# An S5 layer's start reordered: input loaded and squared first, phases rounded through PSUM, turns moved up, Toeplitz products behind all projections

## What is computed

```
def s5_mixer(u, h0, a_re, a_im, log_dt, b_re, b_im, c_re, c_im, d_skip, w_glu):
    lam = lax.complex(a_re, a_im)
    dt = jnp.exp(log_dt)[:, None]
    lam_bar = jnp.exp(lam * dt)
    b_bar = ((lam_bar - 1.0) / lam)[..., None] * lax.complex(b_re, b_im)
    uf = u.reshape(bsz, t_len, SSM_GROUPS, SSM_GROUP)        # u = rmsnorm(x, g_mix)
    bu = einsum('btgh,gph->btgp', uf, b_bar)                 # complex
    if h0 is not None:
        bu = bu.at[:, 0].add(lam_bar * h0)
    _, h = lax.associative_scan(_ssm_combine, (a, bu), axis=1)
    y = einsum(h.real, c_re) - einsum(h.imag, c_im)          # back to 16 channels per group
    y = y.reshape(bsz, t_len, D_MODEL) + d_skip * u
    z = jax.nn.gelu(y)
    gl = z @ w_glu
    return gl[..., :D_MODEL] * jax.nn.sigmoid(gl[..., D_MODEL:]), h[:, -1]
```

## Time and profile before

| | us |
|---|---|
| median of 3 runs | 1636.94 |
| the runs | 1636.31 to 1640.3 |
| profiled execution, as a whole | 1638.2 |
| its span | 1636.4 |

### The profile page before, as it was taken

One profiled execution on the slowest core, in us unless ns is written; L12 is line 12 of the kernel. 1 busy time (PEld: TensorE's weight loads), 2 busy tenths in 40 slices (PEclk: granted clock), 3 DMA queues, 4 the chain that ended last, 5 costly groups with the idle time before them and its releaser, 6 DMA issues.

```text
span 1636.4 us, 23515 instructions
## 1 busy us (share of the span) xinstructions
PE 1510.4 (92%) x8247; PEld 1287.5 (79%) x8248; DVE 1252.6 (77%) x1522; ACT 996.3 (61%) x1299; POOL 121.1 (7%) x142
## 2 busy tenths in 40 slices
PE   2589989999888879999998999998999999999995
PEld 1578989999776868888887888887888888888884
DVE  7844555554656459999987989987999988999993
ACT  3443444433455337777765777766777777777772
POOL 3971103000100000000000000000000000000000
PEclk9589999999988979999999999999999999999997
DMA  2004579544422219999987999987999988999980
GB/s 101 26 1 162 185 130 314 184 170 180 155 102 110 78 51 362 362 364 354 359 321 295 359 374 353 362 324 292 363 370 352 364 345 325 366 365 353 368 328 28
DMA packets 61947, 423.66 MB, mean 259 GB/s; under 512 B 8302, under 2 KB 8454, under 8 KB 11665
## 3 DMA queue, kind: packets, MB, share of 16 engines
q1 hardware_dynamic: 58784, 412.37, 66.8%
q0 software_dynamic: 3056, 9.85, 3.0%
HBM read 415.31 MB, written 6.88 MB: 258 GB/s over the span
## 4 chain that ended last, share of the span: by engine, by line
PE 89%; DVE 7%; ACT 3%; issue 1%; DMA 0%; SPq 0%; DVEq 0%; ACTq 0%
PE ps L1670 26%; PE ps L1672 25%; PE ps L1671 25%; PE ps L1889 2%; PE ps L1902 1%; PE ps L1558 1%; PE ps L1500 1%; PE ps L1589 1%; PE ps L1915 1%; PE ps L1590 1%; PE ps L1536 1%; DVE WL L1178 1%; ACT TM L613 0%; PE ps L1857 0%; DVE rstd L939 0%
## 5 line engine op out<-in xcount | busy, mean ns | idle before, releaser
L1178 DVE TENSOR_TENSOR WL<-raw,WH 128x1024 fp32r<-128x1024 f32 x774 | 906.1, 1222 | 138.5 <-ACT WH L649 138.2
L649 ACT CAST WH<-raw 128x1024 fp32r<-128x1024 f32 x774 | 772.5, 1049 | 181.1 <-PE ps L1672 181.1
L1670 PE MATMUL ps<-WH,XEH 128*128 128x512 f32 x896 | 362.0, 404 | 10.4 <-issue 8.9
L1672 PE MATMUL ps<-WH,XEL 128*128 128x512 f32 x896 | 353.1, 394 | 0.0
L1671 PE MATMUL ps<-WL,XEH 128*128 128x512 f32 x896 | 351.4, 392 | 0.0
L1670 PEld LDWEIGHTS ps<-WH,XEH 128*128 128x128 f32 x896 | 169.3, 189 | 45.5 <-issue 9.3
L1672 PEld LDWEIGHTS ps<-WH,XEL 128*128 128x128 f32 x896 | 169.3, 189 | 42.8
L1671 PEld LDWEIGHTS ps<-WL,XEH 128*128 128x128 f32 x896 | 169.6, 189 | 35.3
L1670 PE MATMUL ps<-WH,AFH 128*128 128x512 f32 x448 | 178.2, 398 | 0.0
L1671 PE MATMUL ps<-WL,AFH 128*128 128x512 f32 x448 | 176.8, 395 | 0.0
L1672 PE MATMUL ps<-WH,AFL 128*128 128x512 f32 x448 | 176.8, 395 | 0.0
(11 more groups left out here) (358 smaller groups left out, 1783.7 us busy)
## 6 DMA issues: line engine op xcount, KB each, us to landing
raw<-in_we SPq DMA_DIRECT2D x336, 1024.0 KB, 5.2
raw<-in_wd SPq DMA_DIRECT2D x51, 1024.0 KB, 4.9
bias_rows<-SC POOLq DMA_DIRECT2D x1, 3072.0 KB, 37.1
BIAS<-bias_rows POOLq DMA_DIRECT2D x16, 128.0 KB, 9.3
U<-in_xu SPq DMA_DIRECT2D x1, 1280.0 KB, 7.2
X<-in_xT SPq DMA_DIRECT2D x1, 1056.0 KB, 9.6
out_yT<-XN SPq DMA_DIRECT2D x2, 528.0 KB, 2.7
out_ks<-KCT POOLq DMA_DIRECT2D x1, 1024.0 KB, 5.1
```

Of the source, the lines that this page charges most:

```text
L649: a.copy(WH[tile[2] % SPLIT][:, cols], raw[slot_][:, cols]).then_inc(sem("hi_made"), 1)
L1178: v.tensor_tensor(WL[tile[2] % SPLIT][:, cols], raw[tile[2] % RING][:, cols], WH[tile[2] % SPLIT][:, cols].bitcast(F32), ALU.subtract).the ...
L1670: t_.matmul(out, sh, mh, start=first, stop=False)
L1672: return t_.matmul(out, sl, mh, start=False, stop=last)
```

## The change

Five edits:
- SP: U and the gain GU are loaded ahead of C and B, instead of behind them.
- ACT: the eight squares of U stand ahead of the sines and the T9 factors, each into a region of its own in CM[1], and without waiting for PE.
- VectorE, `phases`: the step angles are first copied into PSUM bank 0, and the rounding's scratch is PSUM banks 2 and 3 instead of TB.
- VectorE: `turn_back(0, 0)` comes ahead of the second half's `input_side`, the other three after its steps 1, 3 and 5 (before: after 1, 3, 5 and 7); `scale_u(1)` comes after step 3 instead of ahead of all of them.
- PE and ACT: the eight first-half Toeplitz products leave the projection rounds: four follow all of them, two stand behind `swap(1, 0)`, two behind `swap(1, 1)`; `masks(2)`, `masks(3)`, `outputs(0)` to `outputs(2)`, `y_out(0)` and `v_out(1, 3)` move accordingly. PE waits for the phases ahead of the first, since they share banks.

```diff
@@ sync
+            sp.dma_start(U[:, :, :], xu).then_inc(sem("u_loaded"), 16)
+            sp.dma_start(GU[:, :], gu).then_inc(sem("u_loaded"), 16)
             sp.dma_start(CQ[:, :, :], cq[:, 0:GH, :]).then_inc(sem("c_loaded"), 16)
             sp.dma_start(CX[:, :, :], cx[:, 0:GH, :]).then_inc(sem("c_loaded"), 16)
             sp.dma_start(BQ[:, :, :], bq[:, 0:GH, :]).then_inc(sem("b_loaded"), 16)
             sp.dma_start(BX[:, :, :], bx[:, 0:GH, :]).then_inc(sem("b_loaded"), 16)
-            sp.dma_start(U[:, :, :], xu).then_inc(sem("u_loaded"), 16)
-            sp.dma_start(GU[:, :], gu).then_inc(sem("u_loaded"), 16)
@@ scalar
             a.activation(q[3][:, :], q[1][:, :], ACT.Tanh, scale=0.5).then_inc(sem("tanh_ready"), 1)
+            act.wait_ge(sem("u_loaded"), 32)
+            for c in range(8):
+                a.activation(CM[1][:, 3 * c:3 * c + 3, :].rearrange("p a b -> p (a b)")[:, 0:8 * UC],
+                             U[:, 8 * c:8 * c + 8, :].rearrange("p g n -> p (g n)"), ACT.Square)\
+                    .then_inc(sem("u_squared"), 1)
             act.wait_ge(sem("consts"), 5)
             act.wait_ge(sem("phase9_ready"), 1)
...
-            act.wait_ge(sem("u_loaded"), 32)
-            for c in range(8):
-                if c >= 2:
-                    act.wait_ge(sem("squ_summed"), c - 1)
-                a.activation(CM[1][:, 3 * (c % 2):3 * (c % 2) + 3, :].rearrange("p a b -> p (a b)")[:, 0:8 * UC],
...
-                masks(j - 1)
-            masks(3)
+            masks(0)
+            masks(1)
             table_ahead(ACT.Gelu_apprx_tanh)
...
             a_turned(11)
+            masks(2)
             act.wait_ge(sem("scanned"), 2)
             decays(1)
             a_turned(12)
             v_out(1, 1)
             a_turned(13)
-            y_out(0)
+            masks(3)
             a_turned(14)
             v_out(1, 2)
             a_turned(15)
+            y_out(0)
             y_out(1)
+            v_out(1, 3)
             y_out(2)
-            v_out(1, 3)
@@ vector
-                link(v.tensor_tensor(x[:, :, :], q[7][:, gs].unsqueeze(2).to_broadcast([P, GH, NB]),
+                turns8 = ps[:, 0, 0:G]
+                if not hf:
+                    link(v.tensor_copy(turns8, q[7][:, :]))
+                link(v.tensor_tensor(x[:, :, :], turns8[:, gs].unsqueeze(2).to_broadcast([P, GH, NB]),
                                      jramp[:, :].unsqueeze(1).to_broadcast([P, GH, NB]), ALU.mult))
-                part_of_turn(x[:, :, :], TB[:, :, :], sem("phase_ready"))
+                part_of_turn(x[:, :, :], ps[:, 2:4, :].rearrange("p b (g j) -> p (b g) j", j=NB), sem("phase_ready"))
...
-            scale_u(1)
             dve.wait_ge(sem("b_loaded"), 64)
             dve.wait_ge(sem("a_built"), 1)
+            turn_back(0, 0)
             for s in range(L):
                 input_side(1, s)
-                if s % 2:
-                    turn_back(0, s // 2)
+                if s in (1, 3, 5):
+                    turn_back(0, s // 2 + 1)
+                if s == 3:
+                    scale_u(1)
@@ tensor (project, turn_a, project, turn_a, swap in each turn of the loop)
-                if b:
-                    toeplitz(0, b - 2)
-                    toeplitz(0, b - 1)
-            toeplitz(0, 6)
-            toeplitz(0, 7)
+            pe.wait_ge(sem("phase_ready"), 2)
+            for b in range(4):
+                toeplitz(0, b)
             turn_a(1, 0)
...
             swap(1, 0)
+            toeplitz(0, 4)
+            toeplitz(0, 5)
             swap_states(0)
...
             swap(1, 1)
-            outputs(0)
+            toeplitz(0, 6)
+            toeplitz(0, 7)
...
             swap(1, 2)
+            outputs(0)
             outputs(1)
-            outputs(2)
             project(1, 6)
             project(1, 7)
             swap(1, 3)
+            outputs(2)
             outputs(3)
             outputs(4)
```

More of the change, by code:

```diff
@@ L560, in _ @@
             a.activation(T9[1][:, :, :], EI[:, :, :], ACT.Copy, scale=-1.0).then_inc(sem("pow_ready"), 1)
-            act.wait_ge(sem("u_loaded"), 32)
-            for c in range(8):
-                if c >= 2:
-                    act.wait_ge(sem("squ_summed"), c - 1)
-                a.activation(CM[1][:, 3 * (c % 2):3 * (c % 2) + 3, :].rearrange("p a b -> p (a b)")[:, 0:8 * UC],
-                             U[:, 8 * c:8 * c + 8, :].rearrange("p g n -> p (g n)"), ACT.Square)\
-                    .then_inc(sem("u_squared"), 1)
             for c in range(KC):
@@ L1510, in _ @@
                 t_.matmul(ps[:, 7, 0:8 * UC], same[:, :],
-                          CM[1][:, 3 * (c % 2):3 * (c % 2) + 3, :].rearrange("p a b -> p (a b)")[:, 0:8 * UC],
+                          CM[1][:, 3 * c:3 * c + 3, :].rearrange("p a b -> p (a b)")[:, 0:8 * UC],
                           start=(c == 0), stop=(c == 7)).then_inc(sem("squ_summed"), 1)
```

## The result

The changed kernel takes 1647.91 us in the median of 7 runs (1641.93 to 1651.42), the kernel before on the same chip 1637.61 (1636.31 to 1640.3). The ratio is 1.0051, with 95% between 1.0033 and 1.0068: slower by some 8 us (the means of the runs differ by 8.4 us, the two medians by 10.3). The profiled execution took 1648.91 us.

What follows compares the result with a forecast made beforehand. VectorE was taken to bound up to 46.16 us, alternating engines until 97.95, then PE. Front +8.2 and the rest -0.25 on 1638.2 gave 1646.15 profiled, less 1.3: 1644.8 us, range 1631 to 1649.

Steps and rivals of the forecast that it cites:

- forecast A: The prediction's own case: POOL working beside VectorE's SBUF-only chain from 14 to 25 us costs +8.2 us; chance 0.60.
- Part 1: Front, up to the first half of AM: earlier U and squares start POOL earlier, delaying VectorE by 8.2 us.
- the first collision: From 14.14 to 19.80 us: VectorE's 64-column operations wait for POOL's two U*GU products, +4.0 us.
- the case of 14.1 us: If POOL starts U*GU at 14.1 us, two small VectorE operations wait 2.2 us each, +4.5 us.
- the second: From 22.9 to 24.40 us: four or five SBUF-only VectorE operations wait for POOL's output-side products, +4.2 us.
- Part 2: Phases through PSUM: three operations each at 1.22 us plus 0.04; VectorE then idles 2.5 us before the first turn.
- Part 3: Projection rounds with turns moved up: low clock, second-half AM complete at 87.3 us instead of 85.4, a hidden loss.
- Part 4: Toeplitz products behind the projections: second-half projection 5.0 us earlier, four products moved into PE's full stretch; together -0.25 us.
- the second pair: Two more Toeplitz products after the first masks, ending at 88.6 us: 2.5 us, between low-clock and high-clock times.
- Rival B: Projection rounds: the clock rises, rounds take about 4.0 us, -9 us more, whole 1635 to 1637 us; chance 0.14.
- Rival C: Front: costs nothing, as POOL does not hold up such small operations; 1636.7 us, no change; chance 0.12.
- D: Whole kernel: Rival B and Rival C together, or unseen gains in the front; 1627.7 us, faster; chance 0.14.

Runs made afterwards that it cites:

- e1: The changed kernel with one wait: POOL starts all its work only after VectorE's small SBUF-only chain; 1641.05 us, ratio 1.0012 to the kernel before.
- e2: The changed kernel with POOL waiting for the end of VectorE's small SBUF-only chain ahead of its output-side products alone; 1647.33 us in one run.
- e12: The kernel before, unchanged, executed and profiled a second time; 1634.43 us in its one run.
- e8: e1 with four extra products of 128 columns, read by nobody, behind each of the first three swaps; 1629.74 us in one run.
- e9: e7 with four extra products of 128 columns, read by nobody, behind each of the first two swaps; 1627.5 us, ratio 0.9931 to the kernel before.
- e7: The changed kernel with the front as before, GELU table loaded early, and first-half Toeplitz products spread over rounds and second half; 1629.14 us, ratio 0.9947 to the kernel before.

## Why the prediction was right, and where it was not

The prediction said 1644.8 us with 1631 to 1649; it came out at 1647.91 in the median and 1648.91 in the profiled execution, where its sum had 1646.15. The median is within the range, and 0.7 us beyond the 1647.2 that the sum's own bounds gave. The sign and the cause (forecast A) were right. Point by point:

- **Part 1, the front: right.** +8.2 forecast, +8.48 measured, made of three: 0.37 because log_dt took 4.3 us to land instead of 3.9 (VectorE's first operation at 8.00 instead of 7.63, a term that the prediction left out; U's megabyte is now right behind it in the queue, but that this is why was not tested); 4.21 of the first collision (4.0 forecast; two operations over two POOL products, as the case of 14.1 us had it); 3.90 of the second (4.2 forecast; five operations, but the fifth lost only 0.30, since POOL was nearly through). "SBUF — State Buffer" in the Trainium skill, section "SBUF: two separate sides", says that the port pair VectorE and GpSimd share is held for a whole instruction, and that who comes second waits for all of it, VectorE if it reads two SBUF operands or runs in a two-port mode; the trace agrees: 2.33 us for an operation of 0.19 beside a POOL product of 2.33, and 0.36 us, the same as before, for the operation with PSUM operands that stands among the five. Two rows were read too freely: the product of 0.69 us at 28.93 ends before POOL starts at 29.71 (those behind it, with POOL at work, take 0.69 too), and the addition of 0.21 us at 125.94 has a POOL operation beside it that ends at 126.03, so it is no clean case without POOL.
- **Part 2, phases: right.** 1.23 us per operation with PSUM, the rounding too, where 1.25 was taken between 0.7 and 1.25. The rule of "VectorE: DVE Perf Modes" in the Trainium skill, section "Why PSUM operands drop a tier", that an fp32 operation with a PSUM operand runs in no doubled mode, agrees with the trace: 1.23 us for 1024 columns, no faster than the operations with two inputs beside it, while the same rounding in SBUF takes 0.46 us for 576 columns (at 12.74 us) where the one with two inputs behind it takes 0.76. VectorE's idle time ahead of the first turn was 2.75 us, forecast 2.5.
- **Part 3, rounds: right but for one size.** Turns at 67.25, 75.03 and 82.82 us are 7.78 apart, forecast 7.75; the granted clock is 0.50. `scale_u(1)` took 1.85 us, not 2.55: like the one at 59.51 it waited for POOL, but POOL's instruction had only 0.5 us left. AM was complete at 95.17, that is 86.7 on the clock of before, forecast 87.3 (where the sum took 2.35 for `scale_u(1)` and not the 2.55 it names).
- **Part 4, Toeplitz: two misses that cancel.** The projection of the second half came at 102.77, or 94.29 on the clock of before, forecast 92.95: the gain is 3.66 us, not 5.0. Of the 1.3 missing, 0.6 is the second pair (3.11 us where 2.5 was taken, since the granted clock had risen at 92.5 and was at 0.51 again from 96 to 99 us), and 0.7 was lost before ACT's masks began (84.5 on the clock of before, forecast 83.8). Behind it the stretch to GLX took 39.22 us instead of 35.59: +3.63 where the terms gave +4.75, mostly as the pair behind `swap(1, 0)` took 2.38 us instead of 3.3 (the granted clock, 0.50 from 103 to 109.5 us, rose in it). Together -0.03, forecast -0.25.
- **Rival B** fell for this kernel, as the rows said: PE busy 6.30 of 6.30 us at a granted clock of 0.50. "TensorE: Matmul & The Clock Gate" in the Trainium skill, Part 1, says that sustained matmul activity releases the clock; it was not released here, and the measurement decides. **Rival C** fell with e1 and e2: operations of 64 columns are held up. **D** needed both.
- **The rest**: the 2.2 us between +8.45 at GLX and +10.7 at the end are within what two executions of the kernel before differ by (3.7 us, e12). The prediction had allowed 1 or 2 us for that.
- **A slip in the chances**: 0.60 less 0.05 is 0.55 for slower, and not 0.56; nothing hangs on it.

Where the prediction was right as a sum, it was blind as an account, and in Parts 2 to 4 its sum came out by luck. It joined Parts 2 to 4 to -0.25 us and named no part of that as a loss. Taken alone, phases are worth -4.96 and turns -3.72, and the Toeplitz move costs +6.86. The step behind that is the baseline of Part 4: it set the cleared path to the projection against before's, and so never asked what the rounds would be with phases and turns moved but the products left in place. The rows for it were there: before's clock was low from 37.5 to 75 us and rose with the first Toeplitz products in the rounds, which the prediction states under rival B, and uses only against that rival.

## What to carry to other kernels

Work that an engine off the critical path can start earlier is not free: look first at what the engine on the path reads and where, and hold the early one back with one wait if both go to the same port (here one line, 7 us). Products with no hurry that fill the gaps of a waiting TensorE may be what keeps its clock up; before they are moved out, look at the granted clock of the stretch with and without them. Price each edit of a change against the others left out as well as against the kernel before: a sum near zero can be a gain and a loss.

## What the runs showed of the hardware that was not expected

- **PE can be busy all the time at the lower clock.** Projections of 40 columns, turns of AM and swaps kept PE busy 6.30 of 6.30 us, and 7.80 of 7.80 in e8 from 60.4 to 68.2 us, at a granted clock of 0.50. With fillers of 128 columns between them it was 1.00 from 69 to 82 us, though PE was busy only 9.53 of 13.00. Why the fillers raised it and the projections did not is not settled by these runs.
- **Useless work can pay.** e8 and e9 gained 7.3 and 6.1 us at GLX by products that nobody reads; in the time of the whole the gain is not shown beyond e8's one run (e9's interval overlaps e7's).
- **Turn-taking goes down to the shortest operations.** 64 columns cost 2.33 us instead of 0.19, and VectorE got in between two POOL products issued back to back: it waited for one at a time, not for both.
- **A long kernel has chance of its own size.** Up to GLX the kernel before repeats to 0.06 us in two executions; single stages behind it differ by 2.4 to 3.3 us, and the end by 3.7.
